# Down projections as seven products on 2x2 blocks, in two passes of 12 and 10 inner tiles, with two weight sums made by adding DMAs

## The chip, the cores and the metric

One core of a Trainium2 chip runs the kernel. The metric is device time in microseconds of a run; each of the three runs shown before the change took 1123.52, 1124.08 or 1124.08 us, so the median is 1124.08. The other rows come from one profiled execution of the same kernel.

## The reference

The program is a trunk of two layers on x of 512 tokens by 1024 features, in float32. Layer 0 mixes tokens by windowed attention, layer 1 by gated linear attention. After each mixer comes a gated feed-forward block, and the change is in its last matrix product:

```
def conv_ffn(h, w_up, conv_w, conv_b, w_down):      # w_up (1024, 5632), w_down (2816, 1024)
    u = h @ w_up
    gate, up = u[..., :D_FF], u[..., D_FF:]
    gp = jnp.pad(gate, ((0, 0), (CONV_W - 1, 0), (0, 0)))
    conv = conv_b + conv_w[0] * gp[:, 0:S]
    for i in range(1, CONV_W):
        conv = conv + conv_w[i] * gp[:, i:i + S]
    return (jax.nn.silu(conv) * up) @ w_down
...
        x = x + conv_ffn(rmsnorm(x, ffn_norm[i]), f_w_up[i], f_conv_w[i], f_conv_b[i], f_w_down[i])
    return rmsnorm(x, final_norm)
```

## The kernel before, in words

Everything is held transposed: features on the 128 partitions, the 512 tokens along the free dimension. X has 8 feature tiles; the hidden layer has 22 tiles (FT = 22). Products keep nearly full float32 accuracy with single-pass operands: a weight w and an activation a are each split into a high part (a copy rounded to float32r) and a low part (w minus its high part). One tile product is then three matmuls, wh*ah, wh*al and wl*ah (`product`, line 315).

Weights stream through four slots (WH, WL and WRAW, with WRAW and WL in the same place). For each unit, SyncE loads the raw block once the unit that used the slot is done (L243, L256), ScalarE casts it to the high part (`hi`, L678, L743, L747, L758, L762), VectorE subtracts to the low part (`lo`, L1006), and TensorE multiplies. A unit of the up phase is one output tile: 8 inner tiles times 3 matmuls of 512 columns, 24 in all. Unit s writes bank s of four.

An up step (`ffn_step`) handles one hidden tile, and takes a gate unit and an up unit. VectorE evacuates the gate product times R, the inverse RMS (L1044). ScalarE applies the convolution's last tap and bias (c0, L719), VectorE the other two taps (L1048, L1051). ScalarE casts the next weight, then applies silu (L724). GpSimd multiplies by R (the gate, L1360). VectorE multiplies with the up product (AC, L1057). ScalarE casts that to AH (L727), VectorE subtracts to AL (L1059). Each engine executes its instructions strictly in the order written, with waits on semaphores between engines. The steps run in a hardware loop of two steps per iteration (even and odd), and the last two stand written out behind it, where the casts belong to the first down weights.

The down phase has 16 units: 8 output tiles, each in two halves of 11 inner tiles (33 matmuls of 512 columns, 528 in a layer). Unit 0 needs hidden tiles 0 to 10 only. Unit 1 (L362) waits tile by tile for the rest. VectorE then adds the bank to X (`x_add`, L1031); in layer 0 ScalarE makes XH and the square (L707, L708), VectorE XL (L1024), and GpSimd sums the squares (L1350).

At the end of layer 1 the last output tile is computed in two halves of 256 tokens (`last_tile`, L636) so that the final RMSNorm of the first half runs beside the second half's matmuls. `sums` (L647) adds squares on TensorE, ScalarE takes the root (L989), VectorE inverts and builds a diagonal (L1317, L1319), `spread` (L656) spreads it, and VectorE scales six tiles (L1326) and GpSimd two (L1437), which are then stored (L292 to L296).

Of the kernel before, what the change touches and what calls it, by code (L numbers as in the profile page):

```python
# [37 lines left out]
HALF = FT // 2  # L38
# [32 lines left out]

def trunk(nc, xT, gains, w_qkv, sinks, rel_bias, w_o, w_bin, w_ga, w_gate, b_norm, w_bo, w_up, conv_w, conv_b,
          w_down, onehot, ident, causal, causal_pair, out, bias_rows):
    with ExitStack() as ctx:
# [16 lines left out]
        X = place("X", [P, KT_D, T])  # L91
        XH = place("XH", [P, KT_D, T], F32R)
        XL = place("XL", [P, KT_D, T], F32R)
        WH = place("WH", [P, SLOTS, HALF * P], F32R)
        slots_at = place_at[0] + (PHASE - place_at[0]) % ROW
        place_at[0] = slots_at
        WRAW = place("WRAW", [P, SLOTS, HALF * P])
        WL = place("WL", [P, SLOTS, HALF * P], F32R, at=slots_at)
# [3 lines left out]
        SQ = place("SQ", [P, 2, T])  # L102
        ONES = place("ONES", [P, P])
# [23 lines left out]
        region = place_at[0]  # L127


        AH = place("AH", [P, FT, T], F32R)  # L130
        AL = place("AL", [P, FT, T], F32R)
        GS = place("GS", [P, 2, T + 2])
        CV = place("CV", [P, 2, T])
        AC = place("AC", [P, 2, T])
# [17 lines left out]
        place_at[0] += (PHASE - place_at[0]) % ROW  # L152
        fifth_raw_a = place("FIFTH_RAW_A", [P, D])
        fifth_lo_a = place("FIFTH_LO_A", [P, D], F32R, at=place_at[0] - 4 * D)
        fifth_hi_a = place("FIFTH_HI_A", [P, D], F32R)
        end_a = place_at[0]

# [13 lines left out]
        place_at[0] += (PHASE - place_at[0]) % ROW  # L171
        vtt_at = place_at[0]
        VTT = place("VTT", [P, 2, T])
        KS = place("KS", [P, 2, T])
        GAT = place("GAT", [P, T])
        fifth_raw_b = nc.alloc_sbuf_tensor_at("FIFTH_RAW_B", [P, D], F32, offset=vtt_at)
# [4 lines left out]
        ga_at = max(end_a, end_ffn, place_at[0])  # L181
        ga_at += (PHASE - ga_at) % ROW
        GA = place("GA", [P, KT_D, P], F32R, at=ga_at)
        AM = place("AM", [P, 2, 4, P], at=ga_at)
        KUT = place("KUT", [P, 4, P], at=ga_at + 4 * 2 * 4 * P)
        assert ga_at + 8 * KT_D * P <= nc.sbuf_usable_end
# [37 lines left out]
        last_done, last_sq_ready = sem("last_done"), sem("last_sq_ready")  # L224
# [6 lines left out]
        def ksize(u):  # L231

            return HALF if DOWN0 <= u < B_V or u >= DOWN1 else KT_D
# [3 lines left out]
        def _(sp):  # L237
            def load(u, src, k, first=False):

                s = u % SLOTS if isinstance(u, int) else first  # L240
                if not isinstance(u, int) or u >= SLOTS:
                    sp.wait_ge(unit_done, u - SLOTS + 1)
                sp.dma_start(WRAW[:, s, 0:k * P], src).then_inc(raw_landed[s], 16)  # L243
# [6 lines left out]
            def load_all(u0, src, n, k):  # L250

                with sp.Fori(0, n - SLOTS + 1, SLOTS) as i:
                    for s in range(SLOTS):

                        sp.wait_ge(unit_done, i + (u0 + s - SLOTS + 1))
                        sp.dma_start(WRAW[:, s, 0:k * P], src[bass.ds(i + s, 1)].rearrange("a p c -> p (a c)"))\  # L256
                          .then_inc(raw_landed[s], 16)


            sp.dma_start(WRAW[:, 0, 0:D // 2], w_qkv[0, :, 0:D // 2]).then_inc(first_landed, 16)  # L260
            sp.dma_start(X[:, 0:2], xT[:, 0:2]).then_inc(x_landed[0], 16)
            sp.dma_start(WRAW[:, 0, D // 2:D], w_qkv[0, :, D // 2:D]).then_inc(raw_landed[0], 16)
# [3 lines left out]
            for u in range(1, A_O):  # L266
                load(u, w_qkv[u], KT_D)
            for u in range(A_O, A_O + 4):
                load(u, w_o[u - A_O], KT_D)
            load_fifth(A_O + 4, w_o[4])  # L270
            for u in range(A_O + 5, UP0):
                load(u, w_o[u - A_O], KT_D)
            load_all(UP0, w_up[0], 2 * FT, KT_D)
            load_all(DOWN0, w_down[0], 2 * KT_D, HALF)
            load_all(B_V, w_bin, 24, KT_D)
            for u in range(B_O, B_O + 4):
                load(u, w_bo[u - B_O], KT_D)
# [4 lines left out]
            for u in range(B_O + 5, UP1):  # L282
                load(u, w_bo[u - B_O], KT_D)
            load_all(UP1, w_up[1], 2 * FT, KT_D)
            load_all(DOWN1, w_down[1], 2 * KT_D, HALF)
# [16 lines left out]
        def _(pe):  # L302
            mm = nc.tensor.matmul

            def product(s, bank, hi, lo, kbs, wkb, start=True, stop=True, part_ready=None, wh=None, wl=None):

                wh, wl = wh or WH[:, s], wl or WL[:, s]
# [24 lines left out]
            def up_phase(layer, st):  # L332
                u0 = UP[layer]
                for j in range(4):
                    unit(u0 + j, j, XH, XL, part_ready=(xl_ready, KT_D * st))
                    if j == 0:
                        mean_square(st)
                with pe.Fori(4, 2 * FT, 4) as i:
# [3 lines left out]
            def down_unit(u, s, half):  # L342
                pe.wait_ge(lo_ready, u + 1)
                if half == 0:
                    pe.wait_ge(unit_evac, u - 3)
                return product(s, s & 2, AH, AL, range(half * HALF, half * HALF + HALF), 0,
# [1165 lines left out]
```

## Time and profile before

| | before |
|---|---|
| median of 3 runs | 1124.08 us |
| the profiled execution | 1123.7 us |
| its span, first to last instruction | 1121.9 us |
| mean granted TensorE clock | 0.997 of full |
| TensorE / VectorE / ScalarE / GpSimd busy | 98% / 52% / 43% / 14% |
| read from HBM | 99.56 MB |

The span runs from the first to the last instruction, and the profiled execution's own time lies 1.8 us above it. A busy share counts the time in which at least one instruction of the engine was under way. TensorE's matmuls overlap in the records (one of 512 columns is 0.39 us long, but the next starts earlier), so its pace is read from the starts of consecutive ones. "Idle before" is the time in which the engine waited, and the name behind the arrow is what ended it. L is a line of the kernel before.

### The profile page before, as it was taken

The page shows a single profiled execution, that of the slowest core. Times are in us where ns is not written, and L with a number is a line of the kernel's source. Part 1 is how long each engine was busy: PE and PEld are TensorE (multiplying, and loading weights), DVE is VectorE, ACT ScalarE, POOL GpSimd, SP SyncE. Part 2 cuts the span into 40 slices and gives each one's busy share as a digit, 9 for nine tenths or more (in the row PEclk, how much of TensorE's full clock was granted, in tenths as well). Part 3 has the DMA queues.
Part 4 walks back from the last instruction along what each step waited for, and adds up shares of the span by engine and source line. Part 5 has one row for each costly group of instructions (what it writes and reads, how often), then busy time and mean ns, then how long its engine had stood idle before and what let it go on. Part 6 is the DMA issues. An engine that isn't in the chain of part 4 may idle for free.

```text
span 1121.9 us, 14060 instructions
## 1 busy us (share of the span) xinstructions
PE 1099.9 (98%) x5162; PEld 906.0 (81%) x5162; DVE 577.8 (52%) x734; ACT 484.8 (43%) x707; POOL 160.8 (14%) x123
## 2 busy tenths in 40 slices
PE   6999999999999999999999999999999999999996
PEld 5888778888888888888788888778888888888886
DVE  4588565555555553334354556866455555542214
ACT  6366555444454432222652345454544544431211
POOL 6100021111111110001021221121111111110001
PEclk9999999999999999999999999999999999999998
DMA  6511122222222232221222211222222223332212
GB/s 193 160 65 60 36 99 93 100 100 99 93 93 93 101 128 81 100 96 57 79 87 94 80 43 59 84 96 94 93 93 93 93 98 106 108 104 104 84 71 76
DMA packets 31622, 103.48 MB, mean 92 GB/s; under 512 B 3873, under 2 KB 8641, under 8 KB 31586
## 3 DMA queue, kind: packets, MB, share of 16 engines
q1 hardware_dynamic: 27680, 100.68, 26.2%
q10 hardware_dynamic: 3906, 2.31, 1.1%
q8 instruction: 24, 0.39, 0.1%
q14 instruction: 12, 0.10, 0.0%
HBM read 99.56 MB, written 2.88 MB: 91 GB/s over the span
## 4 chain that ended last, share of the span: by engine, by line
PE 89%; DVE 5%; ACT 3%; DMA 1%; POOL 1%; issue 1%; SPq 0%; DVEq 0%; POOLq 0%
PE PS L315 78%; DVE WL L1006 2%; PE PS L636 1%; PE PS L362 1%; PE PS L415 1%; POOL SS L1350 1%; ACT WH L678 1%; PE PS L433 1%; DVE X L1031 1%; ACT SQ L708 1%; PE PS L423 1%; DMA X<-xT 1%; PE PS L547 1%; PE PS L579 0%; PE PS L566 0%
## 5 line engine op out<-in xcount | busy, mean ns | idle before, releaser
L315 PE MATMUL PS<-XH,WH 128*128 128x512 f32 x992 | 393.9, 397 | 9.9 <-DVE XL L1024 9.8
L315 PE MATMUL PS<-XH,WL 128*128 128x512 f32 x992 | 387.2, 390 | 0.0
L315 PE MATMUL PS<-XL,WH 128*128 128x512 f32 x992 | 386.9, 390 | 0.0
L1006 DVE TENSOR_TENSOR WL<-WRAW,WH 128x1024 fp32r<-128x1024 f32 (+1 forms) x169 | 228.9, 1355 | 242.5 <-ACT WH L747 72.0
L315 PEld LDWEIGHTS PS<-XH,WH 128*128 128x128 f32 x992 | 186.7, 188 | 53.5 <-issue 11.8
L315 PEld LDWEIGHTS PS<-XH,WL 128*128 128x128 f32 x992 | 186.6, 188 | 39.6
L315 PEld LDWEIGHTS PS<-XL,WH 128*128 128x128 f32 x992 | 186.8, 188 | 39.2 <-issue 1.7
L1360 POOL TENSOR_TENSOR CV<-CV,R 128x512 f32<-128x512 f32 x44 | 70.5, 1603 | 416.7 <-ACT CV L724 416.7
L315 PE MATMUL PS<-AH,WH 128*128 128x512 f32 x308 | 119.8, 389 | 0.0
L315 PE MATMUL PS<-AL,WH 128*128 128x512 f32 x308 | 119.8, 389 | 0.0
L315 PE MATMUL PS<-AH,WL 128*128 128x512 f32 x308 | 119.8, 389 | 0.0
L678 ACT CAST WH<-WRAW 128x1024 fp32r<-128x1024 f32 (+1 forms) x65 | 70.4, 1083 | 86.1 <-DMA WRAW<-w_bin 56.4
L747 ACT CAST WH<-WRAW 128x1024 fp32r<-128x1024 f32 x40 | 42.0, 1051 | 106.2 <-DMA WRAW<-w_up 106.2
L1350 POOL TENSOR_TENSOR SS<-SS,SQ 128x512 f32<-128x512 f32 x34 | 47.1, 1386 | 222.3 <-ACT SQ L708 219.6
L727 ACT CAST AH<-AC 128x512 f32 (+1 forms) x44 | 27.3, 620 | 114.8 <-DVE AC L1057 114.8
L1057 DVE TENSOR_TENSOR AC<-PS,CV 128x512 f32<-128x512 f32 x44 | 30.4, 692 | 73.1 <-POOL CV L1360 73.1
L315 PEld LDWEIGHTS PS<-AL,WH 128*128 128x128 f32 x308 | 57.8, 188 | 12.1
L315 PEld LDWEIGHTS PS<-AH,WL 128*128 128x128 f32 x308 | 57.8, 188 | 12.0
L315 PEld LDWEIGHTS PS<-AH,WH 128*128 128x128 f32 x308 | 57.8, 188 | 11.9
L1059 DVE TENSOR_TENSOR AL<-AC,AH 128x512 f32 (+1 forms) x44 | 30.5, 693 | 39.4 <-ACT AH L727 39.4
L758 ACT CAST WH<-WRAW 128x1408 fp32r<-128x1408 f32 x12 | 16.5, 1374 | 64.4 <-DMA WRAW<-w_down 64.4
L707 ACT ACTIVATE XH<-X,GAIN 128x512 fp32r<-128x512 f32 (+1 forms) x24 | 17.4, 724 | 60.9 <-DVE X L1031 60.9
(204 smaller groups left out, 1206.3 us busy)
## 6 DMA issues: line engine op xcount, KB each, us to landing
WRAW<-w_up SPq DMA_DIRECT2D x88, 512.0 KB, 3.2
WRAW<-w_down SPq DMA_DIRECT2D x32, 704.0 KB, 4.0
WRAW<-w_bin SPq DMA_DIRECT2D x24, 512.0 KB, 3.2
WRAW<-w_qkv SPq DMA_DIRECT2D x11, 512.0 KB, 4.7
WRAW<-w_o SPq DMA_DIRECT2D x7, 512.0 KB, 3.6
WRAW<-w_bo SPq DMA_DIRECT2D x7, 512.0 KB, 3.3
X<-xT SPq DMA_DIRECT2D x4, 512.0 KB, 6.7
out<-X SPq DMA_DIRECT2D x5, 256.0 KB, 2.2
```

The source lines that it names most:

```text
L315: last = mm(PS[:, bank], w[:, c:c + P], x[:, kb], start=start and n == 0 and w is wh and x is hi, stop=stop and n == len(kbs) - 1 and w is wl)
L362: last = mm(PS[:, 0], w[:, 1, n * P:(n + 1) * P], x[:, kb], start=False, stop=n == HALF - 1 and w is WL)
L678: nc.scalar.copy(WH[:, s, 0:k * P], WRAW[:, s, 0:k * P]).then_inc(hi_ready, 1)
L707: A(XH[:, tile, :], X[:, tile, :], ACT.Copy, scale=GAIN[:, st, tile]).then_inc(xh_ready, 1)
L727: nc.scalar.copy(AH[:, tile, :], AC[:, par:par + 1, :]).then_inc(ah_ready, 1)
L747: nc.scalar.copy(WH[:, s + 1, 0:D], WRAW[:, s + 1, 0:D]).then_inc(hi_ready, 1)
L758: nc.scalar.copy(WH[:, s], WRAW[:, s]).then_inc(hi_ready, 1)
L1006: tt(WL[:, s, 0:k * P], WRAW[:, s, 0:k * P], WH[:, s, 0:k * P].bitcast(F32), ALU.subtract)\
L1057: tt(AC[:, par], PS[:, up], CV[:, par], ALU.mult).then_inc(unit_evac, 1)
L1059: tt(AL[:, tile, :], AC[:, par:par + 1, :], AH[:, tile, :].bitcast(F32), ALU.subtract).then_inc(al_ready, 1)
L1350: nc.gpsimd.tensor_tensor(SS[:], SS[:], SQ[:, par], ALU.add).then_inc(ss_ready, 1)
L1360: nc.gpsimd.tensor_tensor(CV[:, j], CV[:, j], R[:], ALU.mult).then_inc(slr_ready, 1)
```

## The change

It replaces each layer's down projection by Strassen's scheme in the form with seven products and shared sums. Output features, inner tiles and tokens are each split in two: of a pair of output tiles, a pair of inner tiles, and the two halves of 256 tokens. A round makes one pair of output tiles; its seven products Z1, W11, W12, Z2, Z4, Z3, W22 each run over all pairs of inner tiles with 256 columns. The hidden layer is processed in two passes, 12 tiles (6 pairs) and then 10 (5 pairs): up steps of those tiles, then four rounds of down products. Products share PSUM banks: Z2, Z3 and W22 accumulate onto W11's bank and Z4 onto Z1's, and VectorE adds or subtracts the running bank into X after each (`take`). A product on a bank waits for the take before it.

AH and AL hold seven blocks of 256 tokens for each pair: the four plain quarters and three sums, made by VectorE in RW. For the weights, plain quarters are loaded five times a round; Z1's and Z3's raw weights become sums of two quarters by a second DMA, issued by GpSimd, that adds onto the first; Z2's and Z4's are sums made by VectorE (`sum_z2`, `sum_z4`). Each of the seven has its own raw, high and low place. The down weights lie partly over the up slots. The last round of the second pass in layer 1 is followed by the final RMSNorm, whose `sums(0)` stands ahead of the last product and whose other parts stand behind it.

Its core:

```diff
+F0, PAIRS = (0, 12), (6, 5)
...
+ROUNDS = ((("Z1", 0), ("W11", 0), ("W12", 0), ("Z2", 0), ("Z4", 0), ("Z3", 0)),
+          (("Z1", 1), ("W22", 0), ("W11", 1), ("W12", 1), ("Z2", 1), ("Z4", 1), ("Z3", 1)),
+          (("Z1", 2), ("W22", 1), ("W11", 2), ("W12", 2), ("Z2", 2), ("Z4", 2), ("Z3", 2)),
+          (("W11", 3), ("W22", 2), ("Z1", 3), ("Z2", 3), ("Z4", 3), ("Z3", 3), ("W12", 3), ("W22", 3)))
+COUNT = {(4 * chunk + n, name): 28 * chunk + i + 1
+         for chunk in range(4) for i, (name, n) in enumerate(sum(ROUNDS, ()))}
...
+BLOCK = {"W11": 0, "Z1": 1, "Z4": 2, "W12": 3, "Z2": 4, "Z3": 5, "W22": 6}
+END_BANKS = ((4, 5), (6, 2))
...
+SETS = ((4, 5, 6), (7, 0, 1))
...
+        AH = place("AH", [P, PAIRS[0], 7, TH], F32R)
+        AL = place("AL", [P, PAIRS[0], 7, TH], F32R)
+        RW = place("RW", [P, 8, TH])
...
+            def load_up(layer, chunk):
+                u0, n = UP[layer], 4 * (2 * layer + chunk)
+                first, last = 2 * F0[chunk], 2 * (F0[chunk] + 2 * PAIRS[chunk])
+                load_all(u0, w_up[layer], first + (SLOTS if chunk else 0), last - SLOTS)
+                load_down(n, "Z1", "W21")
+                load_down(n, "W11")
+                load_down(n, "W12")
+                for j in range(last - SLOTS, last):
+                    load(u0 + j, w_up[layer, j])
+                sp.wait_ge(unit_done, u0 + last)
+                load_down(n, "Z3", "W11")
+                load_down(n, "W22")
+            def load_round(n, src, next_unit):
+                r = n % 4
+                if r:
+                    sp.wait_ge(down_done, COUNT[n - 1, "Z3"])
+                    load_down(n, "Z3", "W11")
+                if r < 3:
+                    sp.wait_ge(down_done, COUNT[n, "Z1"])
+                    load_down(n + 1, "Z1", "W21")
+                if r:
+                    sp.wait_ge(down_done, COUNT[n - 1, "W22"])
+                    load_down(n, "W22")
+                if r < 3:
+                    sp.wait_ge(down_done, COUNT[n, "W11"])
+                    load_down(n + 1, "W11")
+                    sp.wait_ge(down_done, COUNT[n, "W12"])
+                    load_down(n + 1, "W12")
+                if src is not None and r == 2:
+                    load(next_unit, src[0])
+                    load(next_unit + 1, src[1])
...
-            def down_phase(layer):
-                u0 = DOWN[layer]
-                for s in range(SLOTS):
...
+            def down_product(n, name, bank, start, ready=None):
+                pe.wait_ge(down_lo[name], n + 1)
+                x = BLOCK[name]
+                for kb in range(PAIRS[n // 4 % 2]):
+                    if ready is not None:
+                        pe.wait_ge(al_ready, ready(kb))
+                    c = slice(kb * P, (kb + 1) * P)
+                    for w, act_part in ((DH[name], AH), (DH[name], AL), (DL[name], AH)):
+                        last = mm(PS[:, bank, 0:TH], w[:, c], act_part[:, kb, x],
+                                  start=start and kb == 0 and w is DH[name] and act_part is AH,
+                                  stop=kb == PAIRS[n // 4 % 2] - 1 and w is DL[name],
+                                  skip_group_check=not start)
+                last.then_inc(down_done, 1)
+            def z1(n, ready=None):
+                if n % 4 == 1:
+                    pe.wait_ge(unit_evac, chunk_end(n) - 2)
+                if n % 4 >= 2:
+                    pe.wait_ge(x_taken, COUNT[n - 2, "Z4"])
+                down_product(n, "Z1", SETS[n % 2][2], True, ready)
...
+            def z2(n, ready=None):
+                pe.wait_ge(x_taken, COUNT[n, "W11"])
+                down_product(n, "Z2", SETS[n % 2][0], False, ready)
...
+            def z3(n):
+                pe.wait_ge(x_taken, COUNT[n, "Z2"])
+                down_product(n, "Z3", SETS[n % 2][0], False)
...
+            def down_phase(layer, chunk):
+                n = 8 * layer + 4 * chunk
+                parts = AL_LAYER * layer + AL_COUNT[chunk]
+                z1(n, lambda kb: parts + 2 * kb + 1)
+                w11(n)
+                w12(n, lambda kb: parts + 2 * kb + 2)
+                z2(n, lambda kb: parts + 2 * kb + 2 + (kb == PAIRS[chunk] - 1))
+                z4(n)
+                z3(n)
+                for m in (n + 1, n + 2):
+                    z1(m)
+                    w22(m - 1)
...
             sums(0)
-            last_tile(1, range(5, 10))
+            w22(15)
...
+                if last:
+                    act.wait_ge(unit_evac, u + 2)
+                    nc.scalar.copy(AH[:, kb, 2:4], RW[:, 3:5]).then_inc(ah_ready, 1)
+                    act.wait_ge(t_ready, f + 1)
+                    nc.scalar.copy(AH[:, kb, 4:7], RW[:, 5:8]).then_inc(ah_ready, 1)
+                else:
+                    act.wait_ge(t_ready, f + 1)
+                    pair = after_wait(kb)
+                    if par == 0:
+                        nc.scalar.copy(AH[:, pair, 0:2].rearrange("p o b t -> p (o b) t"), RW[:, 1:3]).then_inc(ah_ready, 1)
+                    else:
+                        nc.scalar.copy(AH[:, pair, 2:7].rearrange("p o b t -> p (o b) t"), RW[:, 3:8]).then_inc(ah_ready, 1)
...
+                weight_hi(n, "W11")
+                ffn_step(layer, f, PAIRS[chunk] - 1, 0, after=lambda: weight_hi(n, "Z1"))
+                weight_hi(n, "Z2")
+                weight_hi(n, "W12")
+                ffn_step(layer, f + 1, PAIRS[chunk] - 1, 1, after=lambda: weight_hi(n, "Z4"), last=True)
...
+                tt(RW[:, 3 * par:3 * par + 2], halves(PS[:, up]), halves(CV[:, par]), ALU.mult).then_inc(unit_evac, 1)
+                dve.wait_ge(unit_evac, u + 2)
+                if par == 0:
+                    stt(RW[:, 2], RW[:, 1], -1.0, RW[:, 0], ALU.mult, ALU.subtract).then_inc(t_ready, 1)
+                    dve.wait_ge(ah_ready, 2 * kb + (parts_before + 1))
+                    tt(parts(AL, 0, 2), RW[:, 1:3], parts(AH, 0, 2).bitcast(F32), ALU.subtract).then_inc(al_ready, 1)
+                    return
+                ah = 2 * kb + (parts_before + 2)
+                tt(RW[:, 5], RW[:, 3], RW[:, 2], ALU.add).then_inc(nt2_ready, 1)
+                tt(RW[:, 6], RW[:, 0], RW[:, 3], ALU.subtract)
+                dve.wait_ge(nt2_ready, kb + ((FT * layer + F0[chunk]) // 2 + 1))
+                stt(RW[:, 7], RW[:, 5], -1.0, RW[:, 4], ALU.mult, ALU.subtract).then_inc(t_ready, 1)
+                dve.wait_ge(ah_ready, ah)
+                if last:
+                    tt(parts(AL, 2, 4), RW[:, 3:5], parts(AH, 2, 4).bitcast(F32), ALU.subtract).then_inc(al_ready, 1)
+                    dve.wait_ge(ah_ready, ah + 1)
+                    tt(parts(AL, 4, 7), RW[:, 5:8], parts(AH, 4, 7).bitcast(F32), ALU.subtract).then_inc(al_ready, 1)
+                else:
+                    tt(parts(AL, 2, 7), RW[:, 3:8], parts(AH, 2, 7).bitcast(F32), ALU.subtract).then_inc(al_ready, 1)
...
+            def sum_z2(n):
+                dve.wait_ge(added["Z1"], 16 * (n + 1))
+                dve.wait_ge(plain["W11"], 16 * (n + 1))
+                if n % 4:
+                    dve.wait_ge(down_done, COUNT[n - 1, "Z2"])
+                c = slice(0, down_cols(n))
+                tt(DRAW["Z2"][:, c], DRAW["Z1"][:, c], DRAW["W11"][:, c], ALU.add).then_inc(summed["Z2"], 1)
...
+            def take(n, name, bank, m, tokens, op, behind=None):
+                dve.wait_ge(down_done, COUNT[n, name])
+                if behind:
+                    dve.wait_ge(x_taken, COUNT[n, behind])
+                x = X[:, 2 * (n % 4) + m, tokens]
+                tt(x, x, PS[:, SETS[n % 2][bank], 0:TH], op).then_inc(x_taken, 1)
...
+            def take_w11(n):
+                take(n, "W11", 0, 0, t1, ALU.add)
...
+                ffn_step(layer, chunk, f, PAIRS[chunk] - 1, 0, mid=lambda: sum_z2(n), after=first_lows)
+                ffn_step(layer, chunk, f + 1, PAIRS[chunk] - 1, 1, mid=lambda: sum_z4(n), after=next_lows, last=True)
+                weight_lo(n, "Z4")
...
+                take_z1(n)
+                take_w11(n)
+                take_w12(n)
+                weight_lo(n, "W22")
+                take_z2(n)
+                weight_lo(n, "Z3")
+                sum_z2(n + 1)
+                weight_lo(n + 1, "Z1")
+                take_z4(n)
+                sum_z4(n + 1)
+                weight_lo(n + 1, "W11")
+                for m in (n + 1, n + 2):
+                    take_z3(m - 1)
+                    weight_lo(m, "W12")
+                    weight_lo(m, "Z2")
+                    take_z1(m)
+                    weight_lo(m, "Z4")
+                    take_w22(m - 1)
+                    if st is not None:
+                        x_lo(st, 2 * (m - 1 - n))
+                    take_w11(m)
...
+            last_square(0, "Z3")
+            take_w12(15)
+            last_inverse(0)
+            take_w22(15)
+            last_square(1, "W22")
+            last_scale(0, range(0, 3))
+            last_inverse(1)
+            last_scale(0, range(3, DVE_TILES))
+            last_scale(1, range(DVE_TILES))
...
+                def add_quarter(n, name, src):
+                    pool.wait_ge(plain[name], 16 * (n + 1))
+                    pool.dma_start(DRAW[name][:, 0:down_cols(n)], quarter(n, src), accum_op=ALU.add)\
+                        .then_inc(added[name], 16)
+                for chunk in range(2):
+                    f0, n = F0[chunk], 4 * (2 * layer + chunk)
+                    with pool.Fori(0, 2 * PAIRS[chunk] - 2, 2) as i:
+                        for j in range(2):
+                            gate(i + (f0 + j), j)
+                    add_quarter(n, "Z1", "W22")
+                    f = f0 + 2 * PAIRS[chunk] - 2
+                    gate(f, 0)
+                    gate(f + 1, 1)
+                    add_quarter(n, "Z3", "W21")
+                    add_quarter(n + 1, "Z1", "W22")
+                    for r in range(1, 4):
+                        if chunk:
+                            sum_square(st + 1, 2 * r - 2)
+                        add_quarter(n + r, "Z3", "W21")
+                        if r < 3:
+                            add_quarter(n + r + 1, "Z1", "W22")
+                        if chunk:
+                            sum_square(st + 1, 2 * r - 1)
```

## Rows read from the trace of the kernel before

**Rows 1.** The page's busy time and share of TensorE and VectorE:

```profile
PE 1099.9 (98%) x5162; PEld 906.0 (81%) x5162; DVE 577.8 (52%) x734; ACT 484.8 (43%) x707; POOL 160.8 (14%) x123
```

**Rows 2.** The chain of waits, pieces in order: start us, length us, what:

```profile
168.28 241.44 PE PS L315 x1065
409.72 7.48 PE PS L362 x33
417.20 104.72 PE PS L315 x462
...
996.55 7.48 PE PS L362 x33
...
1093.79 9.71 PE PS L636 x81
1103.50 0.79 PE PS L647 x8
```

**Rows 3.** The tile AH, TensorE: count, ns min/median/max, first and last start:

```profile
L315 PE MATMUL PS<-AH,WH x308: 389/389/389, 402.1 to 1092.9; 128*128 128x512 f32 x154
```

**Rows 4.** Timeline of VectorE around layer 0's last up steps: start, length, what:

```profile
385.08 1.23 DVE L1006 TENSOR_TENSOR WL<-WRAW,WH 128x1024 fp32r<-128x1024 f32 x1 [1.82 <-ACT WH L747]
387.56 0.69 DVE L1057 TENSOR_TENSOR AC<-PS,CV 128x512 f32<-128x512 f32 x1 [1.25 <-POOL CV L1360]
389.14 0.69 DVE L1059 TENSOR_TENSOR AL<-AC,AH 128x512 f32 x1 [0.89 <-ACT AH L727]
389.75 0.68 DVE L1044 TENSOR_TENSOR GS<-PS,R 128x512 f32<-128x512 f32 x1
...
396.98 1.62 DVE L1006 TENSOR_TENSOR WL<-WRAW,WH 128x1408 fp32r<-128x1408 f32 x1 [2.54 <-ACT WH L678]
399.85 0.69 DVE L1057 TENSOR_TENSOR AC<-PS,CV 128x512 f32<-128x512 f32 x1 [1.25 <-POOL CV L1360]
...
412.14 0.69 DVE L1059 TENSOR_TENSOR AL<-AC,AH 128x512 fp32r<-128x512 f32 x1 [0.69 <-ACT AH L727]
```

**Rows 5.** Timeline of ScalarE, same stretch:

```profile
384.00 1.05 ACT L747 CAST WH<-WRAW 128x1024 fp32r<-128x1024 f32 x1 [2.53 <-DMA WRAW<-w_up]
...
396.84 0.63 ACT L724 ACTIVATE CV<-CV 128x512 f32<-128x512 f32 x1
...
401.10 1.37 ACT L678 CAST WH<-WRAW 128x1408 fp32r<-128x1408 f32 x1
```

**Rows 6.** Timeline of GpSimd, same stretch:

```profile
385.65 1.80 POOL L1360 TENSOR_TENSOR CV<-CV,R 128x512 f32<-128x512 f32 x1 [8.25 <-ACT CV L724]
397.55 2.20 POOL L1360 TENSOR_TENSOR CV<-CV,R 128x512 f32<-128x512 f32 x1 [10.09 <-ACT CV L724]
```

**Rows 7.** Groups by line and shape, VectorE: busy us, mean ns of one:

```profile
L1051 DVE SCALAR_TENSOR_TENSOR CV<-GS,CONVW,CV 128x512 f32<-128x512 f32 x44 | 33.1, 752 | 6.0 <-DVE CV L1048 3.0
```

**Rows 8.** Windows: length, busy time of each engine, granted clock, DMA share, GB/s:

```profile
402.10:521.70 119.60, 119.60 (x529) 99.06 (x528) 38.52 (x35) 32.08 (x34) 11.30 (x8) 1.00 0.27 92
...
1110.90:1121.90 11.00, 1.78 (x13) 1.49 (x12) 5.31 (x12) 0.77 (x2) 1.72 (x2) 0.66 0.47 158
```

**Rows 9.** Timeline of VectorE in the tail:

```profile
1110.98 0.42 DVE L1313 TENSOR_TENSOR X<-PS,X 128x256 f32<-128x256 f32 x1 [0.42 <-PE PS L636]
...
1115.51 3.00 DVE L1326 SCALAR_TENSOR_TENSOR X<-X,GAIN,R 128x256 f32<-128x256 f32 x5
```

**Rows 10.** DMA issues: count, KB each, median us to landing:

```profile
WRAW<-w_up SPq DMA_DIRECT2D x88, 512.0 KB, 3.2
WRAW<-w_down SPq DMA_DIRECT2D x32, 704.0 KB, 4.0
...
WRAW<-w_qkv SPq DMA_DIRECT2D x11, 512.0 KB, 4.7
...
KT<-KT ACTq DMA_DIRECT2D x4, 128.0 KB, 4.7
```

More of the change, by code:

```diff
@@ new lines, in load_chunk @@
+            def load_chunk(n0, src=None, next_unit=0):
+                for n in range(n0, n0 + 4):
+                    load_round(n, src, next_unit)
+                if src is not None:
+                    sp.wait_ge(down_done, COUNT[n0 + 3, "Z3"])
+                    load(next_unit + 2, src[2])
+                    sp.wait_ge(down_done, COUNT[n0 + 3, "W22"])
+                    load(next_unit + 3, src[3])
+            sp.dma_start(WRAW[0][:, 0:D // 2], w_qkv[0, :, 0:D // 2]).then_inc(first_landed, 16)
@@ L330, in mean_square, with after_down @@
                 mm(PS[:, B4], ONES[:], SS[:], start=True, stop=True).then_inc(ms_done, 1)
[L332 to L336, printed above, removed]
+            def after_down(n, s):
+                if s == 0:
+                    pe.wait_ge(x_taken, COUNT[n, "W12"])
+                if s == 1:
+                    pe.wait_ge(x_taken, COUNT[n, "Z4"])
@@ L337, in up_phase @@
+            def up_phase(layer, st, chunk):
+                u0 = UP[layer] + 2 * F0[chunk]
+                for j in range(SLOTS):
+                    if chunk == 0:
+                        unit(u0 + j, j, XH, XL, part_ready=(xl_ready, KT_D * st))
+                    else:
+                        after_down(8 * layer + 3, j)
+                        unit(u0 + j, j, XH, XL)
+                    if chunk == 0 and j == 0:
                         mean_square(st)
-                with pe.Fori(4, 2 * FT, 4) as i:
+                with pe.Fori(SLOTS, 4 * PAIRS[chunk], SLOTS) as i:
@@ L526, in _ @@
             for j in range(16):
+                after_down(7, j)
                 unit(B_V + j, j % 4, XH, XL)
@@ L645, in sums @@
                     tokens = slice((2 * half + j) * P, (2 * half + j + 1) * P)
[L646 to L648 removed]
+                    for i, squares in enumerate((SS, SQ[:, 0], SQ[:, 1])):
+                        last = mm(PS[:, END_BANKS[half][0], j:j + 1], squares[:, tokens], ONES[:, 0:1],
+                                  start=i == 0, stop=i == 2)
                 last.then_inc(ms_done, 1)
@@ L712, in std, with ffn_step @@
                 A(STD[:], PS[:, B4], ACT.Sqrt, bias=EPSC[:], scale=1.0 / D).then_inc(std_ready, 1)
-            def ffn_step(layer, m, par, before=None, after=None):
+            def ffn_step(layer, m, kb, par, after=None, last=False):
                 u, f = UP[layer] + 2 * m, FT * layer + m
@@ L772, in ffn @@
+                hi_unit(u0 + 2 * F0[1] + 3)
+                up_steps(layer, 1)
+                for r in range(4):
+                    down_round(n + 4 + r, st + 1, None if layer else B_V)
+                if layer == 0:
+                    act.wait_ge(x_taken, COUNT[7, "W12"])
+                    x_tile(st + 1, 6)
+                    hi_unit(B_V + 2)
+                    act.wait_ge(x_taken, COUNT[7, "W22"])
                     x_tile(st + 1, 7)
```

511 lines of the change are left out of this document (312 added, 199 removed).

## The prediction

> **What bounds the kernel now.** I read the page's busy shares first: TensorE is busy 98% of the span, VectorE 52% [rows 1]. The chain of waits says the same: from 168.28 us to the end of layer 0's down projection it is one unbroken run of matmuls, and in layer 1 it is again until 1110.9 [rows 2]. So every matmul removed from such a run shortens it, and every wait put into it lengthens it. The rest of the reading asks who is close behind: the order of VectorE, ScalarE and GpSimd in the last up steps, and the tail after the last matmul.
>
> **The matmul stream.** A matmul of 512 columns follows the next after 7.48/33 = 0.227 us; one of 256 columns after 9.71/81 = 0.120 us [rows 2]. Half the columns cost 53%, not 50%. Before, layer 0's down phase runs from 402.1 [rows 3] to 521.9 at its 0.227 a matmul: 528 x 0.2267 = 119.7 us. Layer 1 starts at 996.55 - 7.48 = 989.1 and ends at 1110.9, where VectorE's take follows, 121.8 us [rows 2, 9]; it has 132 short matmuls and the first sums of the end inside. After, a product is 3 matmuls for each of 6 (or 5) pairs, 18 x 0.120 = 2.16 us (1.80), a round of seven 15.1 us (12.6), and a layer 4 x 7 x (18 + 15) = 924 matmuls, 110.9 us. Inside layer 1's run stand also sums of twelve records where 8 took 0.79 us [rows 2]: 1.2 us. Together 241.5 before, 223.0 after: **-18.5 us**.
>
> **The step into the down products.** This is the largest cost. Z2 accumulates onto W11's bank, so it waits until VectorE has taken Z1 and W11, and VectorE takes them only after the whole last up step. Before, that step could be late at no price: the first down unit needs only tiles 0 to 10, and the last tile is not ready until 412.83, 10.7 us after the last up unit ended at 402.1 [rows 3, 4]. Let T be the end of the last up unit. Step costs by rows: VectorE takes 1.22 us for 1024 columns and 1.62 for 1408, so 0.96 for 768 and 1.49 for 1280; 0.69 for 512; 0.75 for a tap; 0.42 for 256; and an independent one behind it starts 0.08 before its end (389.75 against 389.14 + 0.69) [rows 4, 7, 9]. ScalarE takes 1.05 for 1024 and 1.37 for 1408, so 0.84 for 768 and 1.27 for 1280 [rows 5].
> The last step inside the loop (T - 21.8) stays tied to its weight DMA: ScalarE's cast starts 3.7 us after its up unit's end (384.00 against 380.3), GpSimd's gate ends at 387.45 and the product with the up half starts at 387.56, 7.26 us after the unit [rows 4 to 6]. Now it is an odd step: the product 0.65, three 256-column sums 1.15, a 1280-column cast 1.27 and a 1280-column subtraction 1.49, with the hand-overs 11.8 us after the unit, T - 9.9. Next step: gate evacuation and the Z2 sum to T - 8.4, two convolution taps to T - 6.8, silu 0.63, gate 2.2 (what it takes beside a VectorE subtraction), up product, negated sum, cast, subtraction: T - 1.3. Last step: evacuation to T - 0.4, c0 on ScalarE, taps to T + 1.8, silu, gate to T + 4.7, then product, three sums, the low part of blocks 2 and 3 (T + 7.1), of blocks 4 to 6 (T + 8.4), the low part of Z4, and the takes of Z1 and W11, done at T + 9.9. Z2 would otherwise start at T + 6.5 in the first round and T + 5.4 in the second. So TensorE waits 3.4 us, and 4.2 (its shorter tiles give VectorE 0.3 back). Two layers: **+15.2 us**. Bounds: 0 if all of it were hidden, and above, if both gates and both casts are a microsecond later, 4 x 6 = 24.
>
> **Rounds in full flow.** VectorE has per round seven low parts, two sums and seven takes: 9 x 0.96 + 7 x 0.42 = 11.6 of 15.1 us; in the second pass 9 x 0.82 + 2.9 + two low parts of x at 0.75, like a tap [rows 7] = 11.8 of 12.6. ScalarE has about 5.9 and 7.8. They fit, but in the second pass with no slack, and only if data is there. The new thing is the adding DMA of 384 KB, of which no row exists. Nearest rows: 512 KB land 3.2 us after issue, 704 KB in 4.0, 512 KB on a crowded queue in 4.7, 128 KB from SBUF to SBUF in 4.7 [rows 10]. A plain block of 320 to 384 KB is then about 2.6. An adding one moves its block and reads a second: bounds 2.6 and 9 (two crowded transfers one after the other); I take 5, near the 4.7. Of these blocks 7 land in a round where 4 equivalents did, some 180 GB/s against the 92 of before [rows 8]. After Z1 of round m is done, the plain load and the add must be over in 7.7 us in the second pass (VectorE adds Z2's weights there before it takes Z2, and Z3 starts at +9.0), 9.4 in the first; for the last round's Z3, five products after the previous one, 6.7 and 8.4. With 2.6 + 5 only the last round of the second pass is late, 0.9 us a layer: **+1.8 us**. Low end 0; at 9 us, 3 x 3.9 + 4.9 in a second pass and 3 x 2.2 + 3.2 in a first, together 53 us for both layers.
> The Trainium skill gives for this path, in "DMA: Bandwidth & Descriptors", section on the anatomy of one DMA from GpSimd, a fit of 2.0 us plus bytes over 436 GB/s, an estimate of 2.9 us for 384 KB, and the section on the bandwidth ceiling in "Collectives: The Full Stack" says an adding transfer is slow because of its two source reads, not because of the addition; by both an estimate of 3.8 us, and the sum would be 1.8 lower. No row here shows either.
>
> **Around the phases.** Into layer 1's values: ScalarE has a cast of 1.05 between the squares of tiles 6 and 7, and the mean square comes 0.3 late: **+0.3**. Low part of x there has 14 matmuls of cover (3.2 us) before its tile is read. Tail: from the last matmul (1110.9) to the last operation 7.6 us, and 3.4 more to the end [rows 9]. After, VectorE takes W22, squares, scales three tiles of the first half, inverts, and scales three more before the second half's six: last operation at +9.25, where it was 7.6: **+1.65**. Bounds 0 and 3.6 (six scalings of 0.6).
> The remaining edits (new places of tiles, one slot array instead of four, the longer low parts inside the up loop) lie beside TensorE's run: an odd up step grows by 2.7 us on VectorE, whose waits there are for the weight DMA, and four banks let it be 16 us late.
>
> **Sum.** The profiled execution took 1123.7 us (span 1121.9 and 1.8 around it). -18.5 + 15.2 + 1.8 + 0.3 + 1.65 = +0.45: 1124.15; the median of the runs is 0.4 above the profiled one, so 1124.5. Its own range is 1120 to 1129, from the transitions within 1 us each and the adding DMA between 3.5 and 5.5.
>
> **Rivals.** *The step in is mostly hidden.* If the gates run at 1.8 (the loop's row [rows 6]) and ScalarE's casts, no longer waiting for their DMAs, let VectorE come 2 us sooner, each wait is 1 to 1.5 us. For it: the step before the last sits 2.54 us behind a DMA-bound cast and 1.25 behind GpSimd [rows 4]. Against: I have already taken the first of those waits out, and the order on VectorE is fixed. Time: 15.2 becomes 5, 1114 to 1115.
> *The adding DMA is the clock of the rounds.* Place: the Z2 sum on VectorE, which stands in its order ahead of the take of Z2 that the next product waits for. It decides from 5.1 us on. At 6.5: 1.4 x 3 + 2.4 in a second pass, 0.7 in a first, 15 for both layers instead of 1.8, and the Z2 sum in the step in 1 us later, four times: 1124.5 + 17 = 1142. For it: queue traffic doubles, and crowded transfers are the slow rows [rows 10]. Against: DMA engines are busy 27% now.
> *TensorE's clock falls in the new waits.* The granted clock is full through all stretches but after 1110.9, where it averages 0.66 over 11 us, 7.5 us at the lower level of 1.2 GHz, once the dense run had stopped and only short matmuls stood between waits [rows 8]. A fall of that length in each step in costs 3.7 us, 15 in all: 1139. Against: the waits come in two pieces, at most 2.5 us each.
> *Strassen does not save what it says* is settled by rows: 7/8 of the products at 0.120 for 0.227 is 93%, which is in the sum.
>
> **Chances.** Forecast 0.42, hidden step 0.27, slow add 0.25, clock 0.06. Under 0.2% (2.25 us) a measurement of this kernel cannot tell from no change. Of the forecast's 0.42, 0.24 lie inside that, 0.09 below and 0.09 above. So faster 0.36, same 0.24, slower 0.40. The range reaches to the middle of the first rival and into the second: 1113 to 1140.
>
> **What would show it.** Right: matmuls of 256 columns 0.120 us apart through whole rounds; four waits of 3 to 4.5 us in TensorE before the first Z2, ended by VectorE's take; adding DMAs landing about 5 us after the plain one; VectorE over 90% busy in the second pass; a tail of 12.6 us. Wrong: a wait in every round ended by the Z2 sum (the add is slow), no waits before Z2 (I misplaced the last step), product boundaries that cost time of their own, or a clock below full inside the rounds.

## The result and the profile after

The changed kernel takes 1158.28 us (median of 5 runs, 1155.75 to 1161.24), the kernel before on the same chip 1123.71 us: a ratio of 1.0306, interval 1.0295 to 1.0317. It is 34.6 us slower; 1124.5 was predicted, and the time lies outside the range.

The page of the changed kernel first: busy shares, HBM traffic, then the groups that answer to [rows 1, 3].

```profile
span 1159.4 us, 15724 instructions
...
PE 1101.4 (95%) x5896; PEld 942.1 (81%) x5896; DVE 733.4 (63%) x1033; ACT 513.2 (44%) x773; POOL 190.8 (16%) x154
...
HBM read 116.86 MB, written 2.88 MB: 103 GB/s over the span
...
L463 PE MATMUL PS<-AH,DH_Z 128*128 128x256 f32 x352 | 107.2, 304 | 31.4 <-DVE X L1302 31.4
...
L463 PE MATMUL PS<-AH,DH_W 128*128 128x256 f32 x264 | 75.6, 286 | 4.6 <-DVE AL L1264 4.6
...
DRAW_W<-w_down SPq DMA_DIRECT2D x24, 384.0 KB, 5.7
DRAW_W<-w_down SPq DMA_DIRECT2D x24, 320.0 KB, 4.7
DRAW_Z<-w_down SPq DMA_DIRECT2D x16, 384.0 KB, 3.0
DRAW_Z<-w_down POOLq DMA_DIRECT2D x16, 384.0 KB, 6.0
...
DRAW_Z<-w_down SPq DMA_DIRECT2D x16, 320.0 KB, 2.9
DRAW_Z<-w_down POOLq DMA_DIRECT2D x16, 320.0 KB, 5.5
```

The matmuls of the Z products waited 31.4 us for VectorE's take (L1302). Before, the matmuls on AH waited for nothing; the page of before has for them:

```profile
L315 PE MATMUL PS<-AH,WH 128*128 128x512 f32 x308 | 119.8, 389 | 0.0
```

The adding DMA lands 6.0 and 5.5 us after its issue, a plain one of the same tile 3.0 and 2.9, and the plain blocks of DRAW_W, which travel beside the adding ones, 5.7 and 4.7.

The windows of the four down passes and the tail, against [rows 8] (columns as there):

```profile
293.91:365.27 71.36, 64.47 (x505) 63.64 (x504) 45.67 (x69) 23.60 (x30) 8.15 (x8) 0.95 0.57 155
474.10:541.56 67.46, 56.11 (x422) 55.09 (x420) 49.78 (x75) 28.46 (x43) 15.98 (x14) 0.92 0.54 141
899.94:971.12 71.18, 63.23 (x505) 62.20 (x504) 45.99 (x70) 23.97 (x31) 8.18 (x8) 0.98 0.58 156
1079.95:1147.06 67.11, 57.28 (x434) 56.26 (x433) 41.71 (x71) 25.82 (x41) 15.37 (x14) 0.92 0.49 118
1147.06:1159.40 12.34, 3.30 (x22) 2.75 (x20) 8.68 (x19) 0.77 (x2) 3.43 (x4) 0.63 0.51 170
```

The passes take 277.1 us together where the down phases took 241.5: +35.6. The tail takes 12.34 (11.0 before): +1.3. The spans differ by 37.5, so nothing of size is elsewhere. Taking the starts of the 1848 down matmuls one by one, the 277.1 divide into 221.8 of matmuls 0.120 apart, 40.6 of waits, and 14.2 that matmuls 0.213 apart take more than at 0.120; the rest is some 0.1 that each restart behind a wait costs. Of the waits, 14.5 stand in the step in (2.2 to 2.3 before the first Z2 of each pass, 0.8 to 1.7 inside W12), 24.8 before eleven of the sixteen Z3, and 1.25 before the last W22, behind `sums(0)`.

One such Z3 of the second pass, on VectorE, then what GpSimd does meanwhile (timelines):

```profile
500.03 0.82 DVE L1274 TENSOR_TENSOR DL_Z<-DRAW_Z,DH_Z 128x640 fp32r<-128x640 f32 x1 [0.36 <-ACT DH_Z L893]
503.09 0.82 DVE L1283 TENSOR_TENSOR DRAW_Z<-DRAW_Z,DRAW_W 128x640 f32<-128x640 f32 x1 [2.23 <-DMA DRAW_Z<-w_down]
503.84 0.41 DVE L1302 TENSOR_TENSOR X<-X,PS 128x256 f32<-128x256 f32 x1
```

```profile
493.95 0.87 POOL L1720 DMA_DIRECT2D DRAW_Z<-w_down  x1 [1.17 <-DMA DRAW_Z<-w_down]
495.85 0.87 POOL L1720 DMA_DIRECT2D DRAW_Z<-w_down  x1 [1.03 <-DMA DRAW_Z<-w_down]
```

Z1 of the round is done at 492.0. Its plain successor lands at 495.85, and GpSimd issues the adding DMA then, 1.9 us behind the adding DMA for Z3. It lands at 503.05, 7.2 us later (of the kernel's 32 adding DMAs, the twelve that were issued 1.1 to 2.4 us behind another took 5.5 to 8.1 us, the others 4.3 to 6.7). VectorE stands before the Z2 sum (L1283), and behind it in its order stands the take of Z2, which Z3 needs: Z2 was done at 499.2, Z3 could have started at 501.0 and starts at 504.30. That is 11.0 us from Z1's end to the landed sum, where the prediction gave 7.7 as the limit: 3.3 too many, and 3.3 is what Z3 waited.

Behind such a wait (here 2.36 us, round 1 of the first pass) the clock falls; the timeline of TensorE:

```profile
324.52 0.28 PE L463 MATMUL PS<-AH,DL_Z 128*128 128x256 f32 x1
327.00 0.39 PE L463 MATMUL PS<-AH,DH_Z 128*128 128x256 f32 x1 [2.20 <-DVE X L1302]
327.22 0.28 PE L463 MATMUL PS<-AL,DH_Z 128*128 128x256 f32 x1
...
327.94 0.41 PE L463 MATMUL PS<-AH,DH_Z 128*128 128x256 f32 x1
328.15 0.41 PE L463 MATMUL PS<-AL,DH_Z 128*128 128x256 f32 x1
...
330.71 0.41 PE L463 MATMUL PS<-AL,DH_Z 128*128 128x256 f32 x1
330.93 0.34 PE L463 MATMUL PS<-AH,DL_Z 128*128 128x256 f32 x1
```

From 327.73 to 330.93 the starts are 0.213 apart, then 0.120 again: fifteen matmuls at the lower level of 1.2 GHz (granted clock 0.50 in that stretch), 1.4 us lost. The profile's record of the clock shows nine such stretches in the four passes: at the first Z2's wait in each, and behind five of the Z3 waits.

### The profile page after: what moved, and what is told of

It reads as the page before. It is cut to its first block, busy times and chain, and to the rows that moved or that the text cites. A ratio compares the mean times of both kernels' runs of the same rounds, so it can differ in the third digit from the quotient of the medians.

```text
span 1159.4 us, 15724 instructions
## 1 busy us (share of the span) xinstructions
PE 1101.4 (95%) x5896; PEld 942.1 (81%) x5896; DVE 733.4 (63%) x1033; ACT 513.2 (44%) x773; POOL 190.8 (16%) x154
## 4 chain that ended last, share of the span: by engine, by line
PE 36%; DVE 5%; DMA 5%; issue 3%; ACT 3%; POOL 1%; DVEq 0%; POOLq 0%; ACTq 0%
PE PS L417 29%; DMA DRAW_Z<-w_down 4%; PE PS L463 4%; DVE WL L1198 1%; POOL CV L1715 1%; DMA WRAW<-w_up 1%; PE PS L710 1%; ACT WH L833 1%; DVE X L1670 0%; PE PS L742 0%; PE PS L729 0%; DVE DL_Z L1274 0%; DVE RW L1250 0%; PE PS L713 0%; PE PS L744 0%
## 5 line engine op out<-in xcount | busy, mean ns | idle before, releaser
L1198 DVE TENSOR_TENSOR WL<-WRAW,WH 128x1024 fp32r<-128x1024 f32 x137 | 176.7, 1290 | 82.5 <-ACT WH L907 41.4
L463 PE MATMUL PS<-AH,DH_Z 128*128 128x256 f32 x352 | 107.2, 304 | 31.4 <-DVE X L1302 31.4
L463 PE MATMUL PS<-AH,DL_Z 128*128 128x256 f32 x352 | 105.4, 299 | 0.0
L463 PE MATMUL PS<-AL,DH_Z 128*128 128x256 f32 x352 | 105.3, 299 | 0.0
L463 PEld LDWEIGHTS PS<-AH,DH_Z 128*128 128x128 f32 x352 | 73.3, 208 | 34.7 <-DVE X L1302 34.5
L1302 DVE TENSOR_TENSOR X<-X,PS 128x256 f32<-128x256 f32 x112 | 46.4, 417 | 53.4 <-PE PS L463 52.9
L463 PE MATMUL PS<-AH,DH_W 128*128 128x256 f32 x264 | 75.6, 286 | 4.6 <-DVE AL L1264 4.6
L463 PE MATMUL PS<-AL,DH_W 128*128 128x256 f32 x264 | 75.0, 284 | 0.0
L463 PE MATMUL PS<-AH,DL_W 128*128 128x256 f32 x264 | 74.9, 284 | 0.0
L463 PEld LDWEIGHTS PS<-AL,DH_Z 128*128 128x128 f32 x352 | 73.7, 209 | 0.2
L463 PEld LDWEIGHTS PS<-AH,DL_Z 128*128 128x128 f32 x352 | 73.4, 208 | 0.0
L1274 DVE TENSOR_TENSOR DL_Z<-DRAW_Z,DH_Z 128x768 fp32r<-128x768 f32 (+1 forms) x64 | 59.0, 921 | 14.4 <-ACT DH_Z L893 14.3
```

The lines of the kernel that those rows point to most:

```text
L463: last = mm(PS[:, bank, 0:TH], w[:, c], act_part[:, kb, x], start=start and kb == 0 and w is DH[name] and act_part is AH, stop=kb == PAIRS ...
L1198: tt(WL[s][:], WRAW[s][:], WH[s][:].bitcast(F32), ALU.subtract).then_inc(lo_ready, 1)
L1274: tt(DL[name][:, c], DRAW[name][:, c], DH[name][:, c].bitcast(F32), ALU.subtract).then_inc(down_lo[name], 1)
L1302: tt(x, x, PS[:, SETS[n % 2][bank], 0:TH], op).then_inc(x_taken, 1)
```

## The experiments

The table has each kernel's median, its ratio to before with the interval, the length of the four down passes together, and in it the waits and what the lower clock cost (both from the starts of the down matmuls; idle matmuls put in count as waits). The last three columns come from each kernel's one profiled execution, which lay up to 4.3 us off the median. Outside the first row the last column has the 0.1 us of each restart in it: the 1.8, 1.0 and 0.7 of the three kernels with idle matmuls are nothing else, for in their passes the clock record never leaves the full level.

| kernel | us | ratio | passes | waits | low clock |
|---|---|---|---|---|---|
| changed | 1158.3 | 1.0306 (1.0295–1.0317) | 277.1 | 40.6 | 14.2 |
| no second summand | 1128.7 | 1.0029 (1.0016–1.0042) | 247.4 | 17.3 | 8.2 |
| second DMA overwrites | 1138.4 | 1.0126 (1.0107–1.0145) | 255.0 | 23.3 | 9.8 |
| idle matmuls in the waits | 1154.6 | 1.0276 (1.0253–1.0299) | 267.0 | 43.5 | 1.8 |
| silu first | 1179.8 | 1.0497 (1.0478–1.0515) | 279.7 | 45.4 | 12.5 |
| silu first, low part later | 1152.6 | 1.0250 (1.0233–1.0268) | 270.9 | 35.7 | 13.3 |
| sums in DRAM | 1130.7 | 1.0069 (1.0045–1.0092) | 244.1 | 16.8 | 5.5 |
| sums in DRAM, silu first | 1120.6 | 0.9964 (0.9950–0.9978) | 235.5 | 10.3 | 3.3 |
| sums in DRAM, idle matmuls | 1126.0 | 1.0022 (1.0013–1.0031) | 238.7 | 16.0 | 1.0 |
| all three | 1117.1 | 0.9936 (0.9923–0.9950) | 230.3 | 7.9 | 0.7 |

**No second summand.** The plain block stands in for the sum in Z1 and Z3.

```diff
-                    pool.dma_start(DRAW[name][:, 0:down_cols(n)], quarter(n, src), accum_op=ALU.add)\
-                        .then_inc(added[name], 16)
```

> Leaves out the second summand of Z1's and Z3's weights: no adding DMA at all, the casts and the Z2 sum wait for the plain block alone. The rest is the changed kernel. Theory A (the adding DMAs are what the rounds wait for): the waits before Z3 in 11 rounds (24.8 us together) and the stretches at half clock behind them (about 8 us) go, the four waits at the step in (14.6 us) stay: 1125 us. Theory B (VectorE is full in the rounds, the DMA only happens to end last): the waits before Z3 stay within 5 us of what they were, 1153 us or more.

29.6 us go. All Z3 waits but one (1.37 us) are gone, while the step in stays as it was (2.19 to 2.32 before Z2). DRAW_W's blocks land in 3.4 and 3.1. So the adding DMAs caused the Z3 waits and slowed their neighbours. The time is 3.7 us above theory A: the stretches at the lower clock behind the step in got longer (about 8 us in four, about 6 before).

**Second DMA overwrites.** The same bytes from the same queue, but not added.

```diff
-                    pool.dma_start(DRAW[name][:, 0:down_cols(n)], quarter(n, src), accum_op=ALU.add)\
+                    pool.dma_start(DRAW[name][:, 0:down_cols(n)], quarter(n, src))\
```

> The second DMA of Z1 and Z3 is issued by GpSimd at the same place, with the same bytes, but overwrites instead of adding (so the weight sum is left out). Theory A1 (adding is what is slow: two sources read for one written): it lands in 3.5 us instead of 5.5 to 6, plain plus second is 6.5 us, under the 7.7 that a round of the second pass leaves: 1127 us. Theory A2 (seven blocks a round, or GpSimd's queue beside SyncE's, are what is slow): it lands in 5 us or more and the kernel stays at 1150 to 1158 us.

It falls between the two expectations: of the 29.6 us, 9.8 are there again once the second DMA moves its bytes, and 19.8 more only when it adds. The page's rows for them:

```profile
DRAW_W<-w_down SPq DMA_DIRECT2D x24, 384.0 KB, 4.3
...
DRAW_Z<-w_down SPq DMA_DIRECT2D x16, 384.0 KB, 3.0
DRAW_Z<-w_down POOLq DMA_DIRECT2D x16, 384.0 KB, 4.0
```

The blocks of 320 KB of DRAW_W gain nothing from it (4.7 us, as beside the adding DMAs). Adding and overwriting differ in more than the addition. The queue's row of the changed kernel, then of this one (packets, MB, share of 16 engines):

```profile
q0 software_dynamic: 4608, 11.54, 6.1%
```

```profile
q0 software_dynamic: 2560, 11.54, 3.3%
```

The adding DMAs moved the same bytes in nearly twice as many packets. So 19.8 us is the price of the adding DMA as it was issued; no run separates the addition from the packets, or from reading the second summand.

**Idle matmuls in the waits.** 15 of 256 columns into an unused bank ahead of the first Z2 and of each Z3 of rounds 1 to 3; nothing reads them.

```diff
+                for _ in range(15):
+                    mm(PS[:, bank, 0:TH], GA[:, 2], two, start=True, stop=True)
```

> 15 matmuls of 256 columns on constant data into an unused bank stand ahead of each Z2 and Z3 product that waits (15 x 0.120 = 1.8 us, less than each such wait), so TensorE's idle time there is cut to at most 1.5 us. Theory C (idle waits of 2 us and more cost a second time, by a lower granted clock afterwards): the 14 us at half speed go, 1144 us. If the clock falls for another reason, or the records only show slower matmuls by chance: 1158 us. If the fillers delay the products: up to 1165 us.

The lower clock is gone from the passes, so the waits bring it on. The median falls by 3.7 us only. The passes of the two profiled executions differ by 10.1 us, but those are the slowest of the changed kernel (1161.24) and the fastest of this one (1150.82). In all four executions here the granted clock is high (0.993 to 0.996, against 0.980 to 0.985), also in those of 1156.3 and 1157.5 us. So what the faster matmuls gained was lost otherwise there. That it is waited away again before the next Z3, because the adding DMAs set the rounds' pace, fits this, but in the profiled execution only 2.9 us more are waited.

**Silu first.** ScalarE takes the silu before it casts the step's two weights; VectorE makes the second low part at the end of the step.

```diff
                 act.wait_ge(conv_ready, f + 1)
                 A(CV[:, par], CV[:, par], ACT.Silu).then_inc(silu_ready, 1)
+                if first:
+                    first()
```

> Up steps reordered: ScalarE applies silu before the two weight casts, which wait for DMAs, VectorE makes the second low part behind the step instead of ahead of the up product, and Z4's low part comes after the takes of Z1 and W11. Theory D (the step into the down products is late only because each up step is tied to its weight DMA): the waits in the first W12 and before the first Z2 (14.6 us in four) go, and the half-clock stretches behind them (about 6 us): 1138 us. Rival (GpSimd's gate and the long odd step bind the up steps anyway): at most 5 us are gained, 1153 us or more.

21.5 us slower, a miss. Between the profiled executions lie 14.3 us, 2.6 of them in the passes and 11.7 outside. One of TensorE's waits up to layer 0's first down product, of a kind that the changed kernel has none of there (in all, times, longest):

```profile
PE PS L417 <- DVE WL L1196: 3.5, 3, 2.1
```

Low parts of weights come too late in both first up phases (layer 1: 5.3 us), and the first down product starts at 298.7 instead of 293.9. The first passes lose 3 us each, by waits inside their first three products; the second pass of layer 0 gains 3.7. I had moved a low part of 1.25 us behind the step's slowest chain, which is the likely reason.

**Silu first, low part later.** As before, but that low part is made in the next step, while VectorE waits for c0.

```diff
-                        lo(4 * i + (u0 + 2 * j + 5), s + 1)
+                                 mid=lambda: lo(4 * i + (u0 + 2 * j + 3), 3 - s),
```

> As the changed kernel, but ScalarE takes the silu ahead of both weight casts of an up step, and VectorE makes the second weight's low part in the next step, in its slot behind c0, so that the last gate of a pass comes sooner after its matmuls. By the changed kernel's rows the step in costs 14.6 us of waits (2.2 to 2.3 before the first Z2 and 0.9 to 1.4 in W12, at each of four passes) and some 6 us at half clock behind them. Theory A (the step in waits for the chain conv, taps, casts, silu, gate): most of it goes, 1158 - 20 = 1138 us, at least below 1148. Theory B (the chain only moves: the odd up steps are now longer than their 10.9 us of matmuls, as in the run with the silu first): the up phases wait for weights, 1153 us or more.

5.7 us faster than the changed kernel, where 20 were expected. In the second passes the waits in W12 and before the first Z2 are gone, but Z3 of the same round waits 2.0 and 2.6 us instead, and the next two as long as before or longer (up to 3.5), with VectorE's Z2 sum waiting for the adding DMA ahead of them: the adding DMA takes over. In the first passes 1.45 us before Z2 remain. This is neither of the two theories; the next kernels decide it.

**Sums in DRAM.** Z1's and Z3's sums are made ahead of time, by a copy and an adding DMA from DRAM to DRAM, for half of them during the attention and for the rest in the up phases. The rounds load plain blocks only.

```diff
+                sp.dma_start(z_block(n, z), quarter(n, Z_PARTS[z][0])).then_inc(z_copied[k // 8], 16)
...
+                pool.dma_start(z_block(n, z), quarter(n, Z_PARTS[z][1]), accum_op=ALU.add, max_dma_last_dim=2560)\
+                    .then_inc(z_added[k // 8], 16)
```

> As the changed kernel, but the two weight sums Z1 = W21 + W22 and Z3 = W11 + W21 of every round are made ahead of time in DRAM (a copy DRAM to DRAM by SyncE's queue, an adding DMA DRAM to DRAM by GpSimd's, during the attention and the up phases), and the rounds load plain blocks only. Theory A (the adding DMAs inside the rounds set the rounds' pace, 25 us of waits before Z3 and 8 us at half clock): the rounds run as in the run without the second summands, 1129 us, plus at most 4 us for the copies beside the up phases: 1125 to 1133 us. Theory B (the cost is in the bytes and in adding wherever they take place): the moved adds slow the up phases' weight loads, and the time stays above 1145 us.

1130.7, as theory A said. The passes are 3 us shorter than without the second summands, most of it at the lower clock (5.5 us for 8.2). Some 2.6 us are lost outside them (span 1129.0 - 244.1 = 884.9, against 1159.4 - 277.1 = 882.3), and the trace shows where. TensorE waits some 43 us after the start for the small constant loads, the last of them GARAW. The row of this kernel's waits (in all, times, longest):

```profile
PE PS L582 <- DMA GARAW<-w_ga: 2.8, 1, 2.8
```

All four kernels with the copies have this wait (1.8 to 2.8 us), none of the others has it. From 0 to 60 us their DMA share is 0.73 to 0.76, against 0.60.

**Both at once.**

> Both at once: sums made ahead of time in DRAM and the silu ahead of the casts. If both causes are what they are held for and don't overlap, 1158 - 29 - 20 = 1109 us, that is below the kernel before (1124). If the silu order lengthens the up steps, it is no better than the sums in DRAM alone (1129).

1120.6: below the kernel before by 0.36%, though 11 us above the plain sum of what was expected, as the silu order's 20 us were too many. The same silu order that gave 5.7 us with adding DMAs in the rounds gives 10.1 without. In the second passes the matmuls now run without a wait in the step in; of the last pass only the 1.25 us for `sums(0)` remain.

**Sums in DRAM, idle matmuls** (15, before the first Z2 of each pass only).

> The kernel with the sums made ahead in DRAM (1130.7 us), with 15 idle matmuls of 256 columns into an unused bank ahead of the first Z2 of every pass, where TensorE waits 2.2 to 2.3 us; their results are not used. In that kernel the matmuls behind these four waits ran 0.213 us apart instead of 0.120, in all 5.5 us more. Theory A (the fallen clock is a cost of its own, and a wait filled with matmuls does not bring it on): 5.5 us less, 1125 us. Theory B (only the waiting counts: the time at the lower clock is absorbed by the work behind it, as with the filler in the changed kernel, which gave 4 of 12 us back): within 1 us of 1130.7, or above it by what the filler runs past the wait.

1126.0, 4.8 less (by the two ratios to before, 0.47%, or 5.3 us), near the 5.5 of theory A. Where no DMA sets the pace, the fallen clock is a cost of its own.

**All three** (10 idle matmuls in the two passes that still wait).

> The kernel with the sums in DRAM and the silu ahead of the casts (1120.6 us), with 10 idle matmuls of 256 columns ahead of the first Z2 of the two passes where TensorE still waits there (1.5 us; the passes of 12 inner tiles). It had 3.0 us at the lower clock in these two passes, about 1.3 of it behind that wait in one and 1.7 in the other. Theory A: 2 to 3 us less, 1118 us. Theory B: no difference.

1117.05, 7.0 us or 0.6% faster than before, and 3.5 faster than without the idle matmuls. Its passes and tail, windows as above:

```profile
297.66:361.13 63.47, 62.18 (x515) 61.77 (x514) 45.89 (x70) 23.80 (x31) 2.08 (x1) 1.00 0.42 131
469.96:520.54 50.58, 50.58 (x421) 50.42 (x420) 45.55 (x71) 27.15 (x41) 8.48 (x7) 1.00 0.48 143
879.16:943.70 64.54, 62.18 (x515) 61.77 (x514) 47.04 (x72) 25.04 (x33) 2.08 (x1) 1.00 0.41 129
1052.53:1104.24 51.71, 51.71 (x433) 51.71 (x432) 38.63 (x67) 24.46 (x39) 8.28 (x7) 1.00 0.39 109
1104.24:1116.60 12.36, 3.07 (x22) 2.52 (x20) 8.66 (x19) 0.77 (x2) 3.43 (x4) 0.67 0.51 170
```

The clock is full through every pass, and one pass is busy without a gap: 420 matmuls in 50.58 us. The passes take 230.3 us, 11.2 less than the down phases before. The span is only 5.3 shorter: the tail gives back 1.4, and the first down product starts 3.8 us later than in the changed kernel: it has the wait for GARAW too, 2.1 us, and 14 short matmuls behind it at the lower clock (3.01 us, in the other three 1.75).

## Why the prediction was wrong

The profiled execution was forecast at 1124.15 us and took 1161.24. Of the 37 us between, 23 are waits before Z3 and 14 the lower clock; the other terms differ by less than 1 us together.

- **The matmul stream was right.** 0.120 us a matmul, 221.8 us nominal plus 1.25 for `sums(0)` where 223.0 was written. Boundaries between products cost nothing.
- **The step in was right in its waits**: 14.5 us for 15.2, though in two pieces a pass, inside W12 and before Z2, and not in one before Z2. VectorE finished the takes of Z1 and W11 0.2 us sooner than T + 9.9 (Z2 starts at 303.62, T = 293.91). Not in the sum were some 6 us at the lower clock behind these waits.
- **The rounds are the step that failed: the adding DMA, taken as 5 us, measured 6.0 and 5.5, and 7.2 where two lay behind each other.** The sum "2.6 + 5" became 3.65 + 7.2 in the round shown. The mechanism stood among the rivals, with its place and its threshold of 5.1 us. What was mis-sized is the term of 1.8 us: it is 24.8 in waits alone. Two things were missing from it: the plain block ahead takes 3 us and more, and GpSimd issues two adding DMAs 1.9 us apart on one queue, so that the second lands behind the first. With both, Z3 waits in eleven of the twelve rounds behind the first of a pass, where the forecast had one a layer. At that rival's 6.5 us it had priced 15. Leaving the adding DMAs out gives 29.6 us back, moving them away 27.5; overwriting instead of adding gives 19.8.
- **The clock rival, held at 0.06, was right in its mechanism.** It was argued away because waits of at most 2.5 us were thought too short. They were not: 14.2 us went to the lower clock in the changed kernel. That it had priced 15 is luck: it put 3.7 us behind each of the four steps in, which cost some 6 us together, and the other 8 stand behind Z3 waits that it did not have. What filling the waits gives back differs: 3.7 us where the adding DMAs set the pace, 4.8 with the sums in DRAM, where only about a third as much was lost. The two rivals together, 17 and 15 on 1124.5, would have made 1156.5, near the measured time by the same luck.
- **Tail and joins**: +1.3 for 1.65, and nothing else of size for 0.3.
- The estimate of 3.8 us that I drew from the Trainium skill ("DMA: Bandwidth & Descriptors", anatomy of one DMA from GpSimd, with "Collectives: The Full Stack", bandwidth ceiling) is not borne out: overwriting takes 4.0 us where that fit gives 2.9, and adding 6.0. Whether the source reads or the addition are what is slow, no run here shows: the overwriting DMA leaves out the one with the other.

What stays open: whether the copies beside the attention are what makes the small loads late with the sums in DRAM (they go together in every run, but nothing else was varied); why the step in of the first passes keeps 1.45 us in the silu-first order, and how the 19.8 us divide between the longer landing of the adding DMAs and the slower neighbours, and what in the adding DMA costs them.

## What to carry to other kernels

Before you trade matmul time for more operands, follow one round's longest data path (free, load, add, sum, take, next product) with every transfer that shares its queue; a path 1 us over the round is paid in every round. Work off the critical stretch (here sums of weights, which depend on no activation) is cheap only once it is moved out of the loop that waits for it. And once a dense stream gets waits of 2 us, price the clock behind each wait too; matmuls that compute nothing can hold it up where no transfer sets the pace.

## What the runs showed of the hardware

- An adding DMA from DRAM into SBUF of 384 KB lands after 6.0 us (320 KB: 5.5), one that overwrites with the same bytes after 4.0 (3.8). Plain loads of 384 KB beside them take 5.7, 4.3 and, with no second DMA, 3.4 us; those of 320 KB 4.7, 4.7 and 3.1.
- After waits of 2.2 to 3.3 us in a stream of matmuls of 256 columns, some 15 ran 0.213 us apart instead of 0.120; after those of up to 2.04 us in the changed kernel none did. It is no sharp line: in the first pass with the sums in DRAM a wait of 2.32 cost nothing, elsewhere one of 2.04 did, and so did two of 1.35 and 1.46 that began less than 2 us apart (sums in DRAM, silu first). With idle matmuls in the wait the clock stayed full.
- VectorE can be slowed beside GpSimd's own work: the same low part of x took 0.75 us and, with GpSimd's sum of squares beside it, 2.45. Three more in that stretch took 1.5 to 1.9 us, and three with no adding DMA in the kernel 1.55 to 1.7, so that the adding DMAs are not what does it; but some beside a GpSimd operation stayed at 0.75.

```profile
494.35 0.75 DVE L1215 SCALAR_TENSOR_TENSOR XL<-X,GAIN,XH 128x512 fp32r<-128x512 f32 x1
...
496.15 2.45 DVE L1215 SCALAR_TENSOR_TENSOR XL<-X,GAIN,XH 128x512 fp32r<-128x512 f32 x1
```

```profile
496.42 1.63 POOL L1705 TENSOR_TENSOR SS<-SS,SQ 128x512 f32<-128x512 f32 x1
```
